# Attention over a paged cache: one record per page with both layouts, in a ring of seven groups of records

## The reference, cut to what matters

```python
past_c = cache_ckv[page_table].reshape(DB, past_len, KV_LORA)
past_pe = cache_kpe[page_table].reshape(DB, past_len, ROPE_DIM)
...
s = (jnp.einsum('bqhc,bkc->bhqk', ql, kc) + jnp.einsum('bqhr,bkr->bhqk', qp, kpe)).astype(jnp.float32) * scale
s = jnp.where(k_pos[None, None, None, :] <= pos[None, None, :, None], s, -jnp.inf)
p = jax.nn.softmax(s, axis=-1).astype(kc.dtype)
return jnp.einsum('bhqk,bkc->bqhc', p, kc)
```

## Time and profile before

| | us |
|---|---|
| median of 3 runs | 1430.48 |
| lowest and highest | 1430.45, 1430.55 |
| span of the profiled execution | 1428.4 |
| TensorE busy | 1412.2 |
| VectorE, ScalarE, GpSimd busy | 889.8, 742.7, 161.9 |
| median of the runs less the profiled span | 2.1 |

### The profile page before, as it was taken

One profiled execution on the slowest core, in us unless ns is written; L12 is line 12 of the kernel. 1 busy time (PEld: TensorE's weight loads), 2 busy tenths in 40 slices (PEclk: granted clock), 3 DMA queues, 4 the chain that ended last, 5 costly groups with the idle time before them and its releaser, 6 DMA issues.

```text
span 1428.4 us, 29450 instructions
## 1 busy us (share of the span) xinstructions
PE 1412.2 (99%) x11003; PEld 1346.2 (94%) x11003; DVE 889.8 (62%) x1480; ACT 742.7 (52%) x1218; POOL 161.9 (11%) x229
## 2 busy tenths in 40 slices
PE   9999999999999999999999999999999999999998
PEld 9999999999888999999999999999877699999998
DVE  6655535999888675554376555349755548655534
ACT  6555424788646565553265555346533346555423
POOL 0111000010110011110011111001144201111000
PEclk9999999999999999999999999999999999999999
DMA  6444443344242254444434444444599643444441
GB/s 242 163 149 151 153 154 136 119 152 146 100 155 98 89 177 147 147 147 148 147 119 166 154 151 147 154 147 150 187 293 285 212 156 118 169 152 150 147 147 67
DMA packets 50776, 221.01 MB, mean 155 GB/s; under 512 B 6705, under 2 KB 23474, under 8 KB 28802
## 3 DMA queue, kind: packets, MB, share of 16 engines
q1 hardware_dynamic: 38882, 189.07, 38.0%
q0 software_dynamic: 6192, 24.64, 5.2%
q10 hardware_dynamic: 5616, 6.16, 1.3%
HBM read 213.07 MB, written 6.77 MB: 154 GB/s over the span
## 4 chain that ended last, share of the span: by engine, by line
PE 94%; DVE 3%; ACT 2%; issue 1%; DMA 0%; DVEq 0%
PE psum L283 16%; PE psum L287 15%; PE psum L282 15%; PE psum L381 8%; PE psum L380 8%; PE psum L382 8%; PE psum L2681 2%; PE psum L2639 2%; PE psum L309 1%; PE psum L300 1%; PE psum L325 1%; PE psum L304 1%; PE psum L2510 1%; PE psum L311 1%; PE psum L315 1%; PE psum L1553 1%
## 5 line engine op out<-in xcount | busy, mean ns | idle before, releaser
L270 DVE TENSOR_TENSOR w_lo<-raw,w_hi 128x2048 fp32r<-128x2048 f32 x159 | 368.6, 2318 | 290.5 <-ACT w_hi L263 290.4
L263 ACT ACTIVATE w_hi<-raw 128x2048 fp32r<-128x2048 f32 x155 | 296.7, 1914 | 351.7 <-PE psum L382 207.8
L282 PE MATMUL psum<-h_hi,w_hi 128*128 128x320 f32 x1504 | 446.0, 310 | 0.0
L283 PE MATMUL psum<-h_lo,w_hi 128*128 128x320 f32 x1504 | 444.1, 309 | 0.0
L282 PEld LDWEIGHTS psum<-h_hi,w_hi 128*128 128x128 f32 x1504 | 282.1, 188 | 2.6 <-issue 1.3
L283 PEld LDWEIGHTS psum<-h_lo,w_hi 128*128 128x128 f32 x1504 | 283.4, 188 | 0.5
L287 PE MATMUL psum<-h_hi,w_lo 128*128 128x320 f32 x1504 | 251.3, 309 | 0.0
L287 PEld LDWEIGHTS psum<-h_hi,w_lo 128*128 128x128 f32 x1504 | 228.3, 188 | 0.3 <-DVE w_lo L270 0.3
L380 PE MATMUL psum<-hid_hi,w_hi 128*128 (+1 forms) x704 | 217.4, 309 | 0.0
L381 PE MATMUL psum<-hid_lo,w_hi 128*128 (+1 forms) x704 | 217.4, 309 | 0.0
L382 PE MATMUL psum<-hid_hi,w_lo 128*128 (+1 forms) x704 | 217.4, 309 | 0.0
(11 more groups left out here) (459 smaller groups left out, 1957.4 us busy)
## 6 DMA issues: line engine op xcount, KB each, us to landing
raw<-wts SPq DMA_DIRECT2D x161, 1024.0 KB, 4.8
h_plain<-cache_t POOLq DMA_DIRECT2D x44, 160.0 KB, 3.7
h_plain<-cache_t SPq DMA_DIRECT2D x44, 160.0 KB, 3.7
arena<-s POOLq DMA_DIRECT2D x4, 1024.0 KB, 7.2
sgs<-arena POOLq DMA_DIRECT2D x4, 1024.0 KB, 4.6
marena<-cache_t POOLq DMA_DIRECT2D x20, 160.0 KB, 4.0
marena<-cache_t SPq DMA_DIRECT2D x20, 160.0 KB, 3.6
raw<-cache_c SPq DMA_DIRECT2D x16, 128.0 KB, 4.2
```

What stands on the lines that cost most here:

```text
L263: act.activation(w_hi[c0 % 2][:, :], raw_of(c0, pair)[:, :], ACT.Copy).then_inc(hi_ready, 1)
L270: eng.tensor_tensor(w_lo[c0 % 2][:, :], raw_of(c0, pair)[:, :], w_hi[c0 % 2][:, :].bitcast(F32), ALU.subtract).then_inc(lo_ready, 1)
L282: pe.matmul(outs[n], wtile(w_hi, c0, tile0 + n * K + k), src_hi(k), start=(k == 0), stop=False)
L283: pe.matmul(outs[n], wtile(w_hi, c0, tile0 + n * K + k), src_lo(k), start=False, stop=False)
```

## The change: what it does

The host writes one array `cache_tc` in place of `cache_t` and `cache_c`: a page is one record of 128 rows of 576 numbers (288 KB), in a row first the transposed latents and the rotary keys, then the plain latent of a token. One transfer brings a page in both layouts. The page turns on TensorE and the copies on DVE are gone, and ACT issues no pages.

A group is the four records of a unit for one sequence. Unit i uses groups 2i (s = 0, issued by SP) and 2i + 1 (s = 1, issued by POOL). The groups lie in a ring of seven buffers: two in `h_plain`, two in `marena`, three in the space of weight buffers that stand idle during the attention (`page_pool`). For that the weight buffers are laid out anew, and the packed queries (`qpk`), the transposed numerators (`pts`, `ptn`) and `osb` move to other places. From the eighth group on, a load waits for the values of the unit whose buffer it takes. The weight chunk behind the attention is asked for after the values of unit 13 and no longer after those of unit 14. The queries' packing on POOL waits for one chunk more to be split (`lo_ready`).

```diff
-        raw = [sb(f"raw{i}", [P, CHUNK]) for i in range(2)]
-        w_hi = [sb(f"w_hi{i}", [P, CHUNK], F32R) for i in range(2)]
-        w_lo = [sb(f"w_lo{i}", [P, CHUNK], F32R) for i in range(2)]
+        RT = BASE["uk"] % 2
+        s0 = ExitStack()
+        in_pool = [(f"raw{1 - RT}", F32), (f"raw{RT}", F32), (f"w_hi{RT}", F32R), (f"w_lo{RT}", F32R)]
+        wbuf = {name: sb(name, [P, CHUNK], dt, s0) for name, dt in in_pool}
+        s0.close()
+        page_pool = sb("page_pool", [P, 4 * CHUNK])
...
+        REC = PGW + KV_LORA
+        GW = QP * REC
+        NTS, NGB = 3, 7
...
+        gbuf = [a_.rearrange("p (g n) -> p g n", g=QP) for a_ in
+                [h_plain[:, i * GW:(i + 1) * GW] for i in range(2)]
+                + [marena[:, o_ + i * GW:o_ + (i + 1) * GW] for i in range(2)]
+                + [page_pool[:, free0 + i * GW:free0 + (i + 1) * GW] for i in range(3)]]
...
+        def records(i, s):
+            return gbuf[(2 * i + s) % NGB]
...
-        def page_plain_pe(pe, i):
...
         def values_pe(pe, i):
             pe.wait_ge(s_trt, i + 1)
-            pe.wait_ge(c_dve, i + 1)
-            pe.wait_ge(qland[i % 2], (16 if i % 2 == 0 else 0) + 16 * 2 * (i // 2 + 1))
-            pe.wait_ge(spland[i % 2], 16 + 16 * 2 * (i // 2 + 1))
-            pe.wait_ge(ppland[i % 2], 16 * 2 * (i // 2 + 1))
...
-                    last = pe.matmul(bank[V_BANK][rows, 0:KV_LORA], pts[:, g, rows], plain_b[i % 2][g] if s else first_plain(i, g),
+                    last = pe.matmul(bank[V_BANK][rows, 0:KV_LORA], pts[:, g, rows], records(i, s)[:, g, PGW:REC],
                                      start=(g == 0), stop=(g == QP - 1))
                 last.then_inc(pv_page, 1)
...
-                page_plain_pe(pe, n)
...
-                copy_plain(n)
...
         def pack_pool(pool):
-            pool.wait_ge(lo_ready, BASE["uk"] + 1)
+            pool.wait_ge(lo_ready, BASE["uk"] + 2)
...
-        def load_pages(eng, s, land, i):
+        def load_records(eng, s, land, i):
             p, q = i // NQT, i % NQT
-            if i >= NTS:
-                eng.wait_ge(c_tr, i - NTS + 1)
+            j = 2 * i + s
+            if j >= NGB:
+                eng.wait_ge(pv_page, QP * ((j - NGB) // 2 + 1))
+            elif j >= 4:
+                eng.wait_ge(chunk_done, BASE["uk"] + 1)
+                eng.wait_ge(lo_ready, BASE["uk"] + 2)
             for g in range(QP):
                 n = page_of(eng, 2 * p + s, QP * q + g)
-                eng.dma_start(slot[i % NTS][:, g, s, :], io["cache_t"][bass.ds(n, 1), :, :].rearrange("a p n -> p (a n)")) \
+                eng.dma_start(records(i, s)[:, g, :], io["cache_tc"][bass.ds(n, 1), :, :].rearrange("a p n -> p (a n)")) \
                    .then_inc(land[i % NTS], 16)
...
-            load_pages(sp, 0, aland, 0)
-            load_pages(sp, 0, aland, 1)
+            load_records(sp, 0, aland, 0)
             load_chunk(sp, BASE["uk"] + 1)
...
-            for i in range(2, NUN):
-                load_pages(sp, 0, aland, i)
-                load_plain(sp, 0, spland, i - 2)
-            for i in range(NUN - 2, NUN):
-                load_plain(sp, 0, spland, i)
+            for i in range(1, NUN):
+                load_records(sp, 0, aland, i)
+            sp.wait_ge(pv_page, QP * (NUN - 2))
+            load_chunk(sp, BASE["uk"] + 2)
             sp.wait_ge(n_scores, NP)
             sp.wait_ge(s_done, NUN)
-            sp.wait_ge(pv_page, QP * (NUN - 1))
-            load_chunk(sp, BASE["uk"] + 2)
...
-            load_plain(pool, 1, ppland, 0)
-            for i in range(NTS, NUN):
-                load_pages(pool, 1, bland, i)
-                load_plain(pool, 1, ppland, i - 2)
-            for i in range(NUN - 2, NUN):
-                load_plain(pool, 1, ppland, i)
+            for i in range(2, NUN):
+                load_records(pool, 1, bland, i)
```

More of the change, by code:

```diff
@@ L132, in sem @@
             return ctx.enter_context(nc.semaphore(name))
-        raw = [sb(f"raw{i}", [P, CHUNK]) for i in range(2)]
-        w_hi = [sb(f"w_hi{i}", [P, CHUNK], F32R) for i in range(2)]
-        w_lo = [sb(f"w_lo{i}", [P, CHUNK], F32R) for i in range(2)]
+        RT = BASE["uk"] % 2
[4 more added lines that the diff above has]
+        page_pool = sb("page_pool", [P, 4 * CHUNK])
+        wbuf |= {name: sb(name, [P, CHUNK], F32R) for name in (f"w_hi{1 - RT}", f"w_lo{1 - RT}")}
+        raw, w_hi, w_lo = ([wbuf[f"{kind}{i}"] for i in range(2)] for kind in ("raw", "w_hi", "w_lo"))
         con = sb("con", [P, CW])
@@ L2230, in build @@
[L2230 to L2236, removed]
@@ L2237, in build @@
-        o_ += CW_
-        qpe = marena[:, o_:o_ + HEADS // 2 * TOK].rearrange("p (h t) -> p h t", h=HEADS // 2)
[L2239 to L2246, removed]
+        qd = marena[:, o_ + 3840:o_ + 3840 + 4 * TOK].rearrange("p (t n) -> p t n", t=4)
@@ new lines, in build @@
+        Q01 = 2 * NP * P
+        free0 = Q01 + KV_LORA
+        assert 2 * GW + QP * P <= H2 and free0 + 3 * GW <= 4 * CHUNK
+        gbuf = [a_.rearrange("p (g n) -> p g n", g=QP) for a_ in
+                [h_plain[:, i * GW:(i + 1) * GW] for i in range(2)]
+                + [marena[:, o_ + i * GW:o_ + (i + 1) * GW] for i in range(2)]
+                + [page_pool[:, free0 + i * GW:free0 + (i + 1) * GW] for i in range(3)]]
+        o_ += 2 * GW
+        def records(i, s):
+            return gbuf[(2 * i + s) % NGB]
@@ new lines, in build @@
+        qpe = marena[:, o_:o_ + HEADS // 2 * TOK].rearrange("p (h t) -> p h t", h=HEADS // 2)
+        o_ += HEADS // 2 * TOK
+        qpk = [a_.rearrange("p (b q) -> p b q", b=NP) for a_ in
+               (page_pool[:, 0:NP * P], page_pool[:, NP * P:Q01], marena[:, o_:o_ + NP * P])]
+        ptn = marena[0:NSMP, o_ + NP * P:o_ + 2 * NP * P].rearrange("p (b q) -> p b q", b=NP)
+        assert o_ + 2 * NP * P <= AW - H2 - 2 * 2 * HEADS * TOK
+        osb = page_pool[:, Q01:free0]
+        pts = h_plain[:, 2 * GW:2 * GW + QP * P].rearrange("p (g q) -> p g q", g=QP)
@@ L2256, in build @@
         nst = lambda j, p=0, n=1: lnv[:, 128 + 4 * j + p:128 + 4 * j + p + n]
-        aland, spland = first_landed[0], first_landed[1][0:2]
+        aland = first_landed[0]
         bland = [sem(f"bland{i}") for i in range(NTS)]
-        ppland = [sem(f"ppland{i}") for i in range(2)]
         (dq_taken, dq_sq, dq_n, qn_hi, qn_lo, qp_taken, qp_rot, qp_step, qpe_ready, uk_done,
@@ L2628, in scores_pe @@
             p = i // NQT
-            t = slot[i % NTS]
+            t = [records(i, s) for s in range(2)]
             pe.wait_ge(aland[i % NTS], 16 + 16 * QP * (i // NTS + 1))
@@ L2638, in scores_pe @@
                     for s in range(2):
-                        pe.matmul(o[s][f], qpk[:, w, p, s * NSMP:(s + 1) * NSMP],
-                                  t[:, :, s, w * P + f * HP:w * P + (f + 1) * HP], start=(w == 0), stop=False)
+                        pe.matmul(o[s][f], qpk[w][:, p, s * NSMP:(s + 1) * NSMP],
+                                  t[s][:, :, w * P + f * HP:w * P + (f + 1) * HP], start=(w == 0), stop=False)
             for s, f in ((0, 0), (1, 1), (0, 1), (1, 0)):
                 rows = slice(f * ROPE, (f + 1) * ROPE)
-                last = pe.matmul(o[s][f], qpk[rows, 2, p, s * NSMP:(s + 1) * NSMP], t[rows, :, s, 2 * P:PGW],
+                last = pe.matmul(o[s][f], qpk[2][rows, p, s * NSMP:(s + 1) * NSMP], t[s][rows, :, 2 * P:PGW],
                                  start=False, stop=True)
@@ L2746, in transposed @@
                 act.wait_ge(s_tr, i + 1)
-                act.wait_ge(pv_page, QP * i) if i else act.wait_ge(lo_ready, BASE["uk"] + 2)
+                if i:
+                    act.wait_ge(pv_page, QP * i)
                 act.activation(pts, bank[T_BANK][:, :].rearrange("p (g q) -> p g q", g=QP), ACT.Copy).then_inc(s_trt, 1)
```

75 lines of the change are left out of this document (13 added, 62 removed).

## The result

The changed kernel takes 1458.58 us (median of 4 runs, 1455.91 to 1462.77), the kernel before it 1430.51 beside it: ratio 1.0197, 95% interval 1.0179 to 1.0215. It is 28 us slower; the forecast was 7 us slower, and the measured time lies outside the range of 1425.5 to 1444. The profiled execution took 1457.23 us.

The account below looks back on a forecast made before the run. TensorE, busy 1412.2 of 1428.4 us, was taken as the bound, with DMA engines nearly full in the attention. A 6.3 us gain and 13.3 us of waits made +7.0 on 1430.48: 1437.5 us, range 1425.5 to 1444.

Parts of the forecast that it names:

- Gain, 6.3 us: Attention on TensorE: dropping the page transposes saves 6.6 us, less 0.3 in units 3, 7 and 11.
- 15 x 0.44: Page turn on the chain in units 0 to 14, 0.44 us each: 6.6 us removed.
- POOL's group is released one iteration ahead of its need, and its fourth issue comes 4.64 us later: Second sequence's loads: 7.05 us between release and need; fourth issue 4.64 us after release.
- For rows of 2.3 KB I take 325 ... 7.3 us: Eight records, 2.36 MB, pass through the 16 DMA engines at 325 GB/s in 7.3 us.
- 9.1 us from release to landing: POOL's group lands last under even queue shares: 1.7 + 7.3 = 9.0 us, 9.1 with the closing semaphore.
- upper bound of 10.1: POOL's slowest release to landing, from its median landing in the fullest stretch: 10.1 us, giving 1444 us in all.
- 2 us in every second unit, 13.3 us in all: TensorE waits before scores in units 3 to 15: 1.03 us on average over 13 units.
- A drop of the granted clock ... I left it out, since no row here prices it: TensorE's clock after waits: a drop would make the forecast too low; no cost was included.
- Rival 1: POOL's group served first: landing 7.35 us, waits 2 us, 1426.2 us, or 1424.2 without waits; chance 0.25 with rival 2's share.
- Rival 2: DMA transfers become the bound: +2.5 us at 317 GB/s, 1426.7 us, a floor under the wait; chance within rival 1's 0.25.

Follow-up runs that it names:

- e5: Kernel before without the page turn and VectorE's copy, loads and bytes unchanged, part of the result wrong: 1425.43 us, ratio 0.9962.
- e4: Changed kernel without SP's loads of the first sequence's records from unit 4 on, part of the result wrong: 1440.44 us, ratio 1.0070.
- e3: Changed kernel with queues exchanged (SP loads the second sequence, POOL the first); seventh group also waits for unit 0's scores: 1452.13 us, ratio 1.0143.
- e11: e3 without POOL's loads from unit 4 on, so SP's group loads alone, part of the result wrong: 1431.00 us, ratio 0.9998.
- e1: Changed kernel with both queues loading two records of every group, in order of need; seventh group also waits for unit 0's scores: 1432.44 us, ratio 1.0012.
- e7: Changed kernel with a group's four page numbers loaded into registers ahead of the wait for its buffer: 1448.05 us, ratio 1.0129.
- e2b: Changed kernel with 12 products of ones on TensorE ahead of the scores of units 3, 5, ..., 13: 1452.22 us, ratio 1.0150.

## Why the prediction was wrong

The direction and the mechanism were right; two terms of the sum were too small, one of them zero.

- *Gain, 6.3 us:* 5.2 (e5). Of the 1.1 that is missing, 0.44 lies in iteration 1, which took 8.51 us before and in e5 alike: without the turn TensorE comes earlier to L2578 and waits there for VectorE (line below; before, no wait of that kind in this iteration), and 15 x 0.44 counted it. In units 3, 7 and 11 the gain was 0.28 us each, so 0.16 went in each where I had put 0.1. The rest is not placed.

```profile
PE psum L2578 <- DVE sq L2615: 0.3, 1, 0.3
```

- *POOL's group is released one iteration ahead of its need, and its fourth issue comes 4.64 us later:* right, 4.67.
- *"For rows of 2.3 KB I take 325 ... 7.3 us", so 9.1 us from release to landing:* this step failed; it took 10.5 on the mean of the six waits, more than the upper bound of 10.1 too. By the rows of unit 5 the rate was 300 GB/s, and 2.64 MB passed, not 2.36 (over the six: 309 and 2.74, so that the extra bytes weigh more than the rate): I let the burst end before the next release, but a unit is shorter than the burst, so the next group's bytes come in ahead of POOL's last record. That split is read from the trace and was not tested by itself; that company costs is shown: 8.5 us alone (e4). This term by itself gives +17.2, 1447.7, outside the range already.
- *2 us in every second unit, 13.3 us in all:* every second unit is right. The six waits were 3.45 us on the mean, 10.5 - 7.05, as the same rule gives with the measured landing; with the two small ones 22.4 in all.
- *"A drop of the granted clock ... I left it out, since no row here prices it":* it fell, and cost 10.6 us, about half of what the waits cost, on top of them; this is the term that I put at nothing. A bound was at hand from the rows at full clock: if the fall lasts no longer than one iteration, a whole iteration at the half level takes 7.05 us more behind each wait; it took 0.3 to 3.1 more. With the measured terms the sum is -5.2 + 22.4 + 10.6 = +27.8; measured +28.1.
- *Rival 1, POOL served first by its larger packets:* not seen. In the stretch above POOL's packets were 3.7 KB on the mean and SP's 2.1, and POOL's records landed in 5.2 us, SP's in 4.9 (medians); with the queues exchanged (e3) the waits stayed, 21.8 us against 22.4. So the rule of the Trainium skill (DMA: Bandwidth & Descriptors, "Queues, rings and completion order") gave no advantage that these rows show. What fits them better is what the Trainium skill says elsewhere (Trainium Kernel Development and Optimization, "Key Constraints"): the queues of all issuing engines share the same 16 engines, and several issuers save only issue time. e3 agrees; by e4 and e11 SP's group alone came 1.1 us sooner than POOL's, 0.65 of it by earlier issues, and the rest stays open.
- *Rival 2, the transfers as the bound:* as a floor it holds: e1 comes down to 1432.4, 5.7 above the 1426.7 that it gave, and what keeps e1 there stays open.

## What to carry to other kernels

Where one event releases loads with different due times, issue them in the order of need over all queues; a queue for each consumer makes the urgent group land with the patient one. The order, with each group shared by the queues, was worth 26 of 28 us here, with no byte less. When a forecast holds waits of some microseconds on TensorE, price the clock behind them as well, with the half level as the upper bound. And, by the rows of the six waits, a burst that is longer than the time to the next release has to be counted with that release's bytes.

## What was not expected of the hardware

- Four records of 288 KB issued by POOL alone landed 8.5 us behind their release, by SP alone 7.4 (without unit 3), at nearly the same spacing of issues (1.15 and 1.09 us) and with the first issue 0.5 us later on POOL; side by side hardly a difference was left (means of 10.8 and 10.5).
- The same kernel's runs follow the mean granted clock: after at 0.995, 0.992, 0.990 and 0.989 took 1455.9, 1457.2, 1459.9 and 1462.8 us. And a wait alone does not say what the clock does: the changed kernel's wait of 3.33 us in unit 13 was followed by the full clock, that of 3.03 in unit 5 was not; e7's eight waits of 1.1 to 3.1 us cost 1.8 us of clock, e4's seven of 0.9 to 2.9 us the same, and in e2b a wait of 1.95 us behind 2.88 us of products of ones was followed by scores at half speed.
